# Transposes written as four 64x64 products on the quarters of the tensor array, row halves in two neighbouring PSUM banks

## What is computed

```python
# RWKV-7 mixer (8 heads of 64), written as a scan in the reference
sa = einsum('bhvk,bhk->bhv', state, -kk_t)
state = state * w_t + sa[..., None] * (kk_t * a_t) + v_t[..., None] * k_t
y = einsum('bhvk,bhk->bhv', state, r_t)
# sparse attention: 16 query heads, 4 key/value heads, three branches (compressed, selected, window)
pc = masked_softmax(lc, dist_c >= 0); o_c = pc @ vc_blk
ps = masked_softmax(ls, mask_s);      o_s = ps @ v_sel
pw = masked_softmax(lw, mask_w);      o_w = pw @ vwb
out = g0 * o_c + g1 * o_s + g2 * o_w
```

## Time and profile before

| | |
|---|---|
| median of 3 runs | 643.17 us |
| profiled execution | 642.21 us, of which the span of instructions is 640.3 us |
| PE busy | 598.5 us (93% of the span) |
| DVE, ACT, POOL busy | 216.2, 142.9, 19.9 us |
| DMA | 158.95 MB, 248 GB/s on average, over 410 GB/s for most of the last third |

### The profile page before, as it was taken

How to read it: one execution, slowest core, us unless ns; L and a number is a source line. 1 busy time by engine, 2 the same in 40 slices (tenths; PEclk the granted TensorE clock), 3 DMA queues, 4 the chain that set the end, 5 groups by cost and what they waited for, 6 DMA issues and landing times.

```text
span 640.3 us, 11809 instructions
## 1 busy us (share of the span) xinstructions
PE 598.5 (93%) x4968; PEld 432.9 (68%) x4968; DVE 216.2 (34%) x586; ACT 142.9 (22%) x366; POOL 19.9 (3%) x23
## 2 busy tenths in 40 slices
PE   8999999999999999998999999998989888967694
PEld 7988887878877877776788888894434433514241
DVE  3152448625334766357300232334110111011022
ACT  3110234042244443445311000001210111010023
POOL 1000000000200103001000000000000000000000
PEclk9999999999999999999999999999999999979698
DMA  8585344831212121211349993988999999999993
GB/s 313 208 323 173 122 148 155 319 134 67 96 39 69 68 68 68 68 36 41 123 157 425 423 375 131 384 339 334 424 420 419 422 419 421 420 423 419 423 390 125
DMA packets 27415, 158.95 MB, mean 248 GB/s; under 512 B 3024, under 2 KB 7264, under 8 KB 9568
## 3 DMA queue, kind: packets, MB, share of 16 engines
q1 hardware_dynamic: 24352, 137.71, 54.9%
q10 hardware_dynamic: 3008, 20.45, 7.7%
HBM read 157.07 MB, written 1.07 MB: 247 GB/s over the span
## 4 chain that ended last, share of the span: by engine, by line
PE 60%; issue 22%; DMA 6%; SPq 4%; DVE 3%; ACT 2%; POOL 0%; POOLq 0%; DVEq 0%; ACTq 0%
PE bank L620 27%; PE bank L1235 7%; DMA ring<-experts 6%; PE bank L1299 4%; SPq L583 4%; PE bank L1244 4%; PE bank L1308 3%; PE bank L846 3%; PE bank L652 2%; PE bank L955 2%; PE bank L984 2%; PE bank L1004 1%; DVE work L1810 1%; PE bank L968 1%; DMA table<-params 1%
## 5 line engine op out<-in xcount | busy, mean ns | idle before, releaser
L620 PE MATMUL bank<-hT,ring 128*128 128x256 f32 x864 | 199.5, 383 | 0.5 <-ACTq L1447 0.3
L620 PEld LDWEIGHTS bank<-hT,ring 128*128 128x128 f32 x864 | 159.6, 190 | 30.5 <-issue 10.6
L620 PE MATMUL bank<-yT,ring 128*128 128x256 f32 x256 | 55.4, 379 | 0.0
L620 PEld LDWEIGHTS bank<-yT,ring 128*128 128x128 f32 x256 | 48.6, 190 | 6.6
L1299 PE MATMUL bank<-ring,work 128*32 128x512 f32 (+1 forms) x192 | 38.6, 711 | 8.2 <-DMA yT<-experts 6.9
L1810 DVE TENSOR_TENSOR work<-bank,table 128x512 f32<-128x512 f32 (+1 forms) x22 | 11.6, 545 | 98.3 <-PE bank L1244 91.6
L1244 PEld LDWEIGHTS bank<-work,tok 128*128 128x128 f32 x256 | 30.2, 192 | 9.7 <-issue 9.7
L1435 ACT ACTIVATE work<-bank 128x512 f32<-128x512 f32 (+2 forms) x45 | 23.4, 519 | 56.2 <-PE bank L1299 43.6
L1609 ACT ACTIVATE tok<-tok,small 128x128 f32<-128x128 f32 (+1 forms) x64 | 28.4, 445 | 21.7 <-DVE small L2038 20.0
L1244 PE MATMUL bank<-work,tok 128*128 128x128 f32 x256 | 31.5, 278 | 0.5 <-DVEq L2319 0.5
L1308 PE MATMUL bank<-work 128*128 128x512 f32 (+1 forms) x68 | 30.4, 584 | 1.3 <-ACT work L1435 0.7
(11 more groups left out here) (258 smaller groups left out, 730.0 us busy)
## 6 DMA issues: line engine op xcount, KB each, us to landing
ring<-front SPq DMA_DIRECT2D x47, 1024.0 KB, 5.0
ring<-experts SPq DMA_DIRECT2D x40, 1024.0 KB, 22.4
work<-experts SPq DMA_DIRECT2D x9, 1024.0 KB, 27.4
ring<-experts ACTq DMA_DIRECT2D x8, 1024.0 KB, 13.7
table<-experts SPq DMA_DIRECT2D x6, 1024.0 KB, 25.4
yT<-experts SPq DMA_DIRECT2D x6, 1024.0 KB, 26.9
hT<-experts SPq DMA_DIRECT2D x4, 1024.0 KB, 23.5
work<-experts ACTq DMA_DIRECT2D x3, 1024.0 KB, 27.9
```

The lines of the kernel that those rows point to most:

```text
L620: return first(pe.matmul(o, l, r, start=(k == 0), stop=(k == n - 1)))
```

## The change

Three jobs are no longer done by `turned` but by a new `quartered`: the token tiles of the RWKV turn step (b, k, v and a, 32 tiles of 128x128), the compressed probabilities (`cT`, 4 tiles), and the probabilities of those units for which `upper_bank` names a second bank. That is 20 of the 24 units: not those whose step is a scan or the last finish (5, 16, 17, 18). A 128x128 tile becomes four products of a 64x64 block with a 64x64 identity, one on each quarter of the array, and the row half chooses the PSUM bank. All banks become parts of one PSUM tensor, with the plan's numbers permuted over the eight places, so that the pairs (2, 6), (2, 7) and (7, 5) are neighbours and ACT can copy both halves in one instruction. The second bank of a unit is 6 for level, solve and the first finish step and for none, 7 for turn, products, seed and local. It is handed out ahead of the unit's `late` jobs and released by ACT together with the first, after the copy to `probT`. In the turn step the b and k tiles share banks 5 and 6, and the v and a tiles share 5 and 7 and are released together, after ACT's last copy of the three.

```diff
-        bank = [ctx.enter_context(nc.psum_tensor(f"bank{b}", [P, 512], F32)) for b in range(8)]
+        banks = ctx.enter_context(nc.psum_tensor("bank", [P, 8 * 512], F32))
+        seat_of = (0, 1, 5, 2, 3, 7, 4, 6)
+        bank = [banks[:, n * 512:(n + 1) * 512] for n in seat_of]
...
+        def upper_bank(step):
+            if step is None:
+                return 6
+            kind, i, which = step
+            if kind == "scan" or (kind == "finish" and i):
+                return None
+            return 6 if kind in ("level", "solve", "finish") else 7
...
-                hand(f"tok{i}2", 7), hand(f"atok{i}", 5)
+                hand(f"late{i}0", 5), hand(f"late{i}1", 7)
...
-                    hand("cT", 2)
+                    hand("cT", 2), hand("cU", 6)
...
             hand(f"pT{g}{u}", 2)
+            if upper_bank(step):
+                hand(f"pU{g}{u}", upper_bank(step))
             hand_late(step)
...
+            def quartered(names, parts):
+                into = [begin(name) for name in names]
+                for b, part in enumerate(parts):
+                    for c in range(2):
+                        for r in range(2):
+                            rows = slice(64 * r, 64 * r + 64)
+                            to = slice(64 * (c ^ r), 64 * (c ^ r) + 64)
+                            last = pe.matmul(into[r][to, b * DH:(b + 1) * DH], part[rows, to], ident[rows, rows],
+                                             start=True, stop=True)
+                            if c == 1 and b == len(parts) - 1:
+                                end(last, names[r])
...
-                turned(f"pT{g}{u}", [prob[:, n % 2, s * P:(s + 1) * P] for s in (0, 2, 1, 3)])
+                parts = [prob[:, n % 2, s * P:(s + 1) * P] for s in (0, 2, 1, 3)]
+                if f"pU{g}{u}" in plan:
+                    quartered(neighbours(f"pT{g}{u}", f"pU{g}{u}"), parts)
+                else:
+                    turned(f"pT{g}{u}", parts)
...
-                b0 = full(act, f"pT{g}{u}")
-                give(copy(probT[:, n % 2, :], b0[:, :]), "probT_ready", f"pT{g}{u}")
+                if f"pU{g}{u}" in plan:
+                    names = neighbours(f"pT{g}{u}", f"pU{g}{u}")
+                    give(copy(probT[:, n % 2, :].rearrange("p (b r t) -> p r b t", r=2, t=DH), halves_of(names, 0, 256)),
+                         "probT_ready", *names)
+                else:
+                    b0 = full(act, f"pT{g}{u}")
+                    give(copy(probT[:, n % 2, :], b0[:, :]), "probT_ready", f"pT{g}{u}")
```

More of the change, by code:

```diff
@@ L515, in build_layer, with neighbours, both @@
         before_loop = [nth(b) for b in range(8)]
+        def neighbours(*names):
+            return sorted(names, key=lambda name: seat_of[plan[name][0]])
+        def both(names, lo, n):
+            first_, second = (seat_of[plan[name][0]] for name in names)
+            assert second == first_ + 1
+            at = bank[plan[names[0]][0]][:, lo:lo + n]
+            return bass.AP(at.tensor, at.offset, [list(at.ap[0]), [512, 2], [1, n]])
         def full(eng, name):
@@ L793, in early @@
                         pe.wait_ge(q["rwkv_ready"], 1)
-                    for w_, src in enumerate((bf, kf)):
-                        turned(f"tok{i}{w_}", [src[:, m, ts] for m in range(4)])
+                    quartered((f"tok{i}0", f"tok{i}1"), [src[:, m, ts] for src in (bf, kf) for m in range(4)])
                 elif kind == "products":
@@ L856, in late @@
                 if kind == "turn":
-                    turned(f"tok{i}2", [mix[:, 8 + m, ts] for m in range(4)])
-                    turned(f"atok{i}", [ar[:, m, i, 0, :] for m in range(4)])
+                    quartered(neighbours(f"late{i}0", f"late{i}1"), [mix[:, 8 + m, ts] for m in range(4)] +
+                              [ar[:, m, i, 0, :] for m in range(4)])
                 elif kind == "seed":
@@ L1009, in turn_compressed @@
             def turn_compressed():
-                turned("cT", [cpads[:, 256 * i + P * b:256 * i + P * (b + 1)] for b in range(2) for i in range(NT)])
+                quartered(neighbours("cT", "cU"), [cpads[:, 256 * i + P * b:256 * i + P * (b + 1)] for b in range(2) for i in range(NT)])
             pe.wait_ge(q["q_ready"], 4)
@@ L1440, in _, with give @@
             count = {}
-            def give(ins, name, job):
+            def give(ins, name, *jobs):
                 count[name] = count.get(name, 0) + 1
@@ L1446, in give, with halves_of @@
                 act.wait_ge(q[name], count[name])
-                act.sem_inc(bank_free[plan[job][0]], 1)
+                for job in jobs:
+                    act.sem_inc(bank_free[plan[job][0]], 1)
+            def halves_of(names, lo, n):
+                for name in names:
+                    full(act, name)
+                return both(names, lo, n).rearrange("p r (b t) -> p r b t", t=DH)
             def to_hT(n):
@@ L1562, in early @@
                 if kind == "turn":
-                    for w_, dst in enumerate((btok, ktok)):
-                        b0 = full(act, f"tok{i}{w_}")
-                        give(copy(dst, b0[:, :]), "tok_ready", f"tok{i}{w_}")
+                    for r in range(2):
+                        b0 = full(act, f"tok{i}{r}")
+                        give(copy(t1[:, :, :].rearrange("p c (n r t) -> p (c n) r t", r=2, t=DH)[:, :, r, :],
+                                  b0[:, :].rearrange("p (b t) -> p b t", t=DH)), "tok_ready", f"tok{i}{r}")
                 elif kind == "level":
@@ L1578, in late @@
                 if kind == "turn":
-                    b0 = full(act, f"tok{i}2")
-                    give(copy(vrow, b0[:, :]), "tok_ready", f"tok{i}2")
-                    b0 = full(act, f"atok{i}")
+                    names = neighbours(f"late{i}0", f"late{i}1")
+                    give(copy(vrow.rearrange("p (b r t) -> p r b t", r=2, t=DH), halves_of(names, 0, 256)), "tok_ready")
+                    rows_ = halves_of(names, 256, 256)
                     for c in range(2):
-                        ins = copy(rhs[64 - 64 * c:128 - 64 * c, :, 0, :],
-                                   b0[64 * c:64 * c + 64, :].rearrange("p (h v) -> p h v", h=RH))
-                    give(ins, "tok_ready", f"atok{i}")
+                        ins = copy(rhs[64 - 64 * c:128 - 64 * c, :, 0, :].rearrange("p (b r) v -> p r b v", r=2),
+                                   rows_[64 * c:64 * c + 64, :, :, :])
+                    give(ins, "tok_ready", *names)
                 elif kind == "solve":
@@ L1613, in turned_compressed @@
             def turned_compressed():
-                b0 = full(act, "cT")
-                give(copy(cprobT, b0[:, :].rearrange("p (b i t) -> p b i t", b=2, i=NT)), "cprobT_ready", "cT")
+                flat_ = cprobT[:, :, :, :].rearrange("p b i t -> p (b i t)")
+                give(copy(flat_.rearrange("p (b r t) -> p r b t", r=2, t=DH), halves_of(neighbours("cT", "cU"), 0, 256)),
+                     "cprobT_ready", "cT", "cU")
             def gate_tanh(gates):
@@ L2030, in logits @@
                 if n >= 2:
-                    b, cnt_ = plan[f"pT{(n - 2) // 6}{(n - 2) % 6}"]
-                    dve.wait_ge(bank_full[b], cnt_ + 1)
+                    for w_ in "TU":
+                        if f"p{w_}{(n - 2) // 6}{(n - 2) % 6}" in plan:
+                            full(dve, f"p{w_}{(n - 2) // 6}{(n - 2) % 6}")
                 nb, w = (4, P) if u < 2 else (2, S)
```

## The result

The changed kernel takes 666.65 us (median of 4 runs, 663.21 to 668.65), the kernel before 643.13 beside it: 1.035 times the time, 95% interval 1.0325 to 1.0374. So it is 23.5 us slower; the forecast was 13.5, and the measured time lies outside its range. The four executions lie 5.4 us apart, and the interval makes the 23.5 a loss of 20.9 to 24.1, so a difference of another run to this kernel is sure to about 1.6 us only. The profiled execution took 667.42 us; its span (first to last instruction) is 665.5, 25.2 more than before.

A forecast was written before the change was run, and what follows sets the result against it. PE's own list was taken to bound the interleaved stretch; new bank waits and burst costs summed to 13.5 us, giving 655.7 on the profiled execution and 656.7 for the median. The range ran from 650.5 to 662.

The forecast's parts named there:

- What bounds the kernel: From 172 to 330 us only PE's own list sets the time; PE is busy 155.04 of 158 us.
- The burst itself: Quartered tile 0.116 us against 0.109 transposed; a burst costs +0.38 among full-size matmuls, +0.09 behind 64x64 products.
- The new waits: PE's X and xu wait for ACT's probability copy, turn steps and compressed probabilities for banks; release taken as 0.1 us.
- The eight places with a forecast wait: Units 0, 12 1.61 each; 1 0.62; 3 0.56; 11 1.14; 6 2.43; tile 0's turn 1.13; compressed probabilities 1.16 us.
- Units 10 and 14: Bank waits repeating those of units 1 and 3: 0.62 us in unit 10, 0.56 in unit 14.
- Without a new wait remain units 2, 4, 8, 9, 13, 15 ... and units 7, 20, 22, 23 ... In 19 and 21: Burst cost only: first six units 0.54 us together, next four 1.52; 19 and 21 nothing, as PE waits there anyway.
- the experts' stretch: From 330 us to the end: moves as a block with what is before it, as long as before.
- Waits mostly hidden: Interleaved stretch: ACT copies early enough that only PE's bursts count, 4.7 us, so 648; chance 0.08.
- Absorbed or overpaid downstream: Experts' stretch returns up to 8.2 us (648.5, chance 0.05), or more than it is given (636 at full size, 0.05).
- Only two quarters at a time: In the bursts only two array quarters run at once, 0.232 us a tile, up to 665; chance 0.04.
- The first rival's sum: 11 bursts at 0.09, 7 at 0.38, about 0.5 in each of two turn steps: 4.7 us.

The follow-up runs named there:

- experiment 5: The kernel before with one PSUM tensor and quartered probabilities only in the nine units where no new wait was seen: 644.97 us (1.0027).
- experiment 4: The changed kernel, but ACT copies the transposed probabilities before the next unit's exponentials: 659.79 us (1.026).
- Experiment 3: The changed kernel with the seed step's (unit 9) second bank 6 instead of 7: 661.45 us (1.0298).
- Experiment 8: The changed kernel with ACT copying probabilities first, the seed step's second bank 6, and unit 19 transposed as before: 652.16 us (1.0133).
- experiment 9: Experiment 8's kernel with token tiles and compressed probabilities also transposed as before: 649.36 us (1.0089).
- experiment 10: Experiment 9's kernel run again unchanged, as base for experiments 11 and 12: 649.39 us (1.0091).
- experiment 11: Experiment 9's kernel with unit 13's probabilities transposed too: 648.22 us (1.0075).
- experiment 12: Experiment 9's kernel with SP's load loop written out and the ring's load 31 held until ACT has copied unit 13's probabilities: 646.98 us (1.0055).
- experiment 6: The kernel before with only the banks in one PSUM tensor and their places permuted: 642.84 us (0.9997).
- experiment 1: The changed kernel with only the probabilities quartered; token tiles and compressed probabilities transposed as before: 661.17 us (1.0283).

## Why the prediction was wrong

**What bounds the kernel** held: PE's list sets the time of the interleaved stretch, and the change lengthened it mostly by standing still. Both parts were taken too small: 10 us of standing still and 3 to 4 of work were forecast, 15.0 and 7.2 came, 1.8 of the latter by unit 9's clock.

**The burst itself** held: 0.116 us a tile, +0.38 among full-size matmuls, the same figures after, and experiment 5 measured 1.8 us for nine bursts against 2.0.

**The new waits** held in kind. All the places named are there; experiment 4 showed that X and xu wait because ACT's copy comes behind its exponentials. Their size was taken too small: "the release is one more semaphore instruction, so I take 0.1, an estimate". At X, Z and xu it is 0.30 to 0.35 (185.17 to 185.47 in unit 0), in the turn steps 0.17 to 0.19, and 0.34 behind DVE's addition at the compressed probabilities. ACT's release, and then a wait instruction of PE for each bank of a pair, lie in between; no run tells their shares apart. The eight places with a forecast wait came out 1.65 us dearer than forecast, and these releases make up 1.45 of it. Units 10 and 14 were said to repeat units 1 and 3; they cost 0.93 more together, 0.4 of it the same releases; the rest was not followed up.

**"Without a new wait remain units 2, 4, 8, 9, 13, 15 ... and units 7, 20, 22, 23 ... In 19 and 21"** is the step of the prediction that failed: it puts units 9 and 19 at next to nothing. I asked of each second bank which later job would wait for it, and not from whom it had to be taken over. For unit 9 that is A110, the products of unit 8, which DVE holds through its masks: 2.97 us, and 1.83 for the half clock and what went with it, 4.80 against 0.09. Experiment 3 gives 5.2 us back by taking the other bank. For unit 19 it is gup1, the gate of the last finish step, which DVE frees after an addition and the multiplication by that gate: PE starts 1.47 us late, 1.40 against nothing.

```profile
324.04 0.69 PE L990 MATMUL bank<-table,tok 64*64 64x64 f32 x32 [1.47 <-issue]
```

```profile
322.46 0.69 DVE L1865 TENSOR_TENSOR yT<-yT,work 128x512 f32<-128x512 f32 x1
323.19 0.69 DVE L1865 TENSOR_TENSOR yT<-yT,bank 128x512 f32<-128x512 f32 x1
```

The row says `issue`, not DVE: 0.16 us after the end of DVE's second instruction at 323.88 PE starts, so I read it as a wait for the release behind that. Experiment 8 took unit 19 out together with others, so its share alone is read from the trace, not measured. Unit 8 is a third case of the same kind, with `gup0`; it shows only where ACT copies first (experiments 4, 8 to 12). The step that failed is 6.1 us of the profiled pair's 25.2, more than half of the 11.7 that the forecast lacked.

**Before and behind.** The profiled execution was 1.27 us late before any changed instruction. The kernels of the study differ there without a change to the code that runs by then (the `cs` products' last start lies between 139.88 and 141.20 us; in the two profiles of one kernel, experiments 9 and 10, 0.4 us apart), and experiment 6 excludes the banks' places. I expected the experts' stretch to move as a block; it took 1.65 us more, with other moments of half clock. The windows above show that all of it is busy time of PE. Whether it belongs to the change stays open, but it need not: in experiment 6, where only the banks' places differ, the same stretch took 1.1 us more than in the kernel before, in experiment 5 1.9 more, and in experiments 1 and 3 0.5 and 0.2 less, though far more was changed there.

The account of the profiled pair: 13.5 + 4.7 (unit 9) + 1.4 (unit 19) + 1.65 (the eight places) + 0.93 (units 10, 14) + 0.27 (unit 13, 0.18 of it the stop that experiments 9 to 12 follow up) - 0.16 (unit 7) + 1.27 + 1.65 = 25.2.

**The rivals.** Waits mostly hidden: no. Absorbed or overpaid downstream: no, the experts' stretch gave nothing back. Only two quarters at a time: no, the records lie 0.015 us apart in the mean. (The first rival's sum leaves out one of the bursts, 0.4 us at most; it changes nothing.) What came was of the forecast's own kind, waits for banks, and larger than the forecast's range allowed for.

## What to carry to other kernels

When a job gets a second buffer from a shared plan, read both sides of the hand-over for every use: who must release it to you, and who waits until you release it. On an engine that works in order each of these is a wait ahead of all its later work. Small products on quarters of the array pay their way in and out (0.09 to 0.38 us here), so they want to stand beside their own kind. Where a consumer does other work before it empties a bank, moving the emptying first is cheap to try: it won 6.9 us here and 1.6 us without the change. And more instructions are a cost of their own: look at where their packets come when a large load runs.

## What the runs showed that I had not expected

A load of data can make PE stand still, by my reading because it holds up the supply of PE's instructions. Where the 1 MB load of the ring was under way, the packet of instructions came at its very end, at 270.5 instead of 267.4 us, and PE stood still until 2.3 us after the packet. The kernel before has a packet behind this load too, at 267.2, and no stop; a tile on quarters takes eight records of PE where a transpose takes one (the changed kernel 5780 matmul records against 4968 and 48 instruction packets against 41), so PE reaches the end of what it has sooner. That this is why the kernel before goes free is my reading; the runs show only that moving the load takes the stop away. Nor does a trace say for which engine a packet is.

In experiment 8 the same stop was followed by a clock at half level: 1.78 us, then 0.79 us for a matmul that takes 0.38.

```profile
276.61 0.54 PE L990 MATMUL bank<-table,tok 64*64 64x64 f32 x10 [1.78 <-issue]
277.07 0.79 PE L644 MATMUL bank<-hT,ring 128*128 128x256 f32 x1
```

That execution took 656.9 us, the other five of the kernel 651.5 to 652.6. One and the same kernel does both: behind the stop of 1.58 us in experiment 9's profile the granted clock stays 1.00, behind that of 1.61 us in experiment 10's it falls 1.5 us later. So a stop is followed by a lower clock in one execution and not in another, and its price is its length only at the least: 2.97 us cost 4.80 in unit 9.
